# Full-array products for the sample tokens, and the sample states' updates from operands split into rounded halves

## The reference

```python
num   = einsum('btsh,bshv->bthv', qk, vc) + w_inter * einsum('bthk,bhkv->bthv', qc, C)   # within 8 tokens, plus the old state
C_new = sc_prev * C + einsum('bsh,bshk,bshv->bhkv', sc, kc, vc)                          # 128 x 256, one for each b and h
h     = rmsnorm(num / den) ; y = (h * gate) @ w_out
```

## Time and profile before

| | us |
|---|---|
| median of three runs | 2357.36 |
| the profiled execution, its own time | 2356.68 |
| its span, first to last instruction | 2354.9 |
| PE busy in it | 2318.1 (98%) |
| DVE busy | 1079.0 (46%) |
| ACT busy | 670.7 (28%) |
| POOL busy | 29.7 (1%) |

### The profile page before, as it was taken

The page is one execution under the profiler, slowest core; times in us unless marked ns, Lnnn a source line. Parts: engine busy times, 40 slices in busy tenths (PEclk is TensorE's granted clock), DMA queues, the critical chain, the costliest instruction groups (busy, mean ns, idle before and its releaser), DMA issues.

```text
span 2354.9 us, 39247 instructions
## 1 busy us (share of the span) xinstructions
PE 2318.1 (98%) x17176; PEld 2277.5 (97%) x17176; DVE 1079.0 (46%) x1395; ACT 670.7 (28%) x814; POOL 29.7 (1%) x20
## 2 busy tenths in 40 slices
PE   7999999999999999999999999999999999999997
PEld 7999999998989999999999999999988899999997
DVE  5333334684545433333543333354665454334245
ACT  4212222453423222212422222233322432222122
POOL 0000000000000000000000000000000100000000
PEclk9999999999999999999999999999999999999999
DMA  4222222233322222221222222222122222222221
GB/s 174 89 89 72 89 72 72 90 98 107 112 94 75 89 90 72 89 89 63 88 82 90 72 89 89 67 78 90 53 90 76 94 75 92 84 89 72 90 68 62
DMA packets 72551, 201.28 MB, mean 85 GB/s; under 512 B 7268, under 2 KB 26980, under 8 KB 72448
## 3 DMA queue, kind: packets, MB, share of 16 engines
q1 hardware_dynamic: 72448, 199.80, 26.4%
HBM read 187.82 MB, written 11.95 MB: 85 GB/s over the span
## 4 chain that ended last, share of the span: by engine, by line
PE 91%; DVE 4%; issue 3%; ACT 1%; POOL 0%; DMA 0%; DVEq 0%; SPq 0%; POOLq 0%; ACTq 0%
PE ps L443 82%; PE ps L668 3%; PE ps L523 1%; PE ps L710 1%; DVE w_lo L1508 1%; PE ps L688 1%; DVE og L1675 0%; PE ps L699 0%; PE ps L546 0%; PE ps L533 0%; PE ps L717 0%; PE ps L702 0%; DVE x L2159 0%; PE ps L494 0%; POOL scratch L1488 0%
## 5 line engine op out<-in xcount | busy, mean ns | idle before, releaser
L443 PE MATMUL ps<-xn_hi,w_hi 128*128 128x288 f32 x3328 | 718.9, 298 | 12.7 <-DVE w_lo L1508 11.5
L443 PE MATMUL ps<-xn_hi,w_lo 128*128 128x288 f32 x3328 | 713.0, 296 | 0.0
L443 PE MATMUL ps<-xn_lo,w_hi 128*128 128x288 f32 x3328 | 712.8, 296 | 0.0
L443 PEld LDWEIGHTS ps<-xn_hi,w_hi 128*128 128x128 f32 x3328 | 536.6, 189 | 21.9 <-DVE w_lo L1508 11.5
L443 PEld LDWEIGHTS ps<-xn_lo,w_hi 128*128 128x128 f32 x3328 | 536.6, 189 | 0.0
L443 PEld LDWEIGHTS ps<-xn_hi,w_lo 128*128 128x128 f32 x3328 | 536.6, 189 | 0.0
L1096 ACT ACTIVATE w_hi<-raw 128x1024 fp32r<-128x1024 f32 x332 | 331.4, 1046 | 361.1 <-PE ps L443 327.3
L1508 DVE TENSOR_TENSOR w_lo<-raw,w_hi 128x1024 fp32r<-128x1024 f32 x332 | 393.4, 1226 | 39.7 <-ACT w_hi L1096 37.6
L443 PE MATMUL ps<-h_lo,w_hi 128*128 128x288 f32 x1616 | 351.4, 297 | 2.6 <-DVE h_hi L1821 2.6
L443 PE MATMUL ps<-h_hi,w_hi 128*128 128x288 f32 x1616 | 351.8, 297 | 1.4 <-DVE w_lo L1508 1.4
L1553 DVE TENSOR_TENSOR scratch<-ps,rstd 128x576 f32<-128x576 f32 x88 | 66.6, 757 | 537.2 <-PE ps L443 534.2
(11 more groups left out here) (235 smaller groups left out, 1544.4 us busy)
## 6 DMA issues: line engine op xcount, KB each, us to landing
raw<-in_w_gate SPq DMA_DIRECT2D x88, 512.0 KB, 3.7
raw<-in_w_up SPq DMA_DIRECT2D x88, 512.0 KB, 4.5
raw<-in_w_down SPq DMA_DIRECT2D x64, 512.0 KB, 3.8
raw<-in_w_mix SPq DMA_DIRECT2D x64, 512.0 KB, 4.2
raw<-in_w_down SPq DMA_DIRECT2D x32, 384.0 KB, 3.6
state_s<-in_state_c SPq DMA_DIRECT2D x4, 1024.0 KB, 7.1
out_c_s<-state_s SPq DMA_DIRECT2D x4, 1024.0 KB, 4.5
state_s<-in_state_g SPq DMA_DIRECT2D x4, 1024.0 KB, 7.1
```

The source lines that it names most:

```text
L443: ins = nc.tensor.matmul(o, a, b[:, c] if c is not None else b, start=first and j == 0, stop=last and j == 2)
```

## The change

Three things are changed on PE, and the work that feeds them on ACT, POOL and DVE.

1. The 64 x 64 sample products become 128 x 128 or 128-row ones. The score block of `pairwise` is computed for 128 x 128 tokens, of which 64 x 64 are used. `sample_numerator` and `sample_den` contract over all 128 rows; the attention's rows 64 to 127 in those columns are zeros that POOL writes once for each mixer.
2. `sample_updates` takes float32r operands. ACT copies the 64 value rows, rounded, to both halves of a 128-row tile `vs_hi`; POOL writes the rest to the upper rows of `vs_lo`, whose lower rows are zero. POOL writes the keys rounded to rows 0 to 63 of `k_hl` and the rest to rows 64 to 127, and multiplies that by the mask over 128 rows. PE makes two matmuls for each sequence, by `vs_hi` and by `vs_lo`, instead of one float32 product.
3. `head_sums` makes two products of 288 columns instead of 512 and 64, and DVE reads both with one instruction instead of two.

```diff
-    batch = (s // DEC_SEQ == np.arange(DEC_BATCH)[None, :]).astype(np.float32)
+    batch = (s % SAMPLE // DEC_SEQ == np.arange(DEC_BATCH)[None, :]).astype(np.float32)
...
             def pairwise(bank, bank_s, left, right):
-                    ins = nc.tensor.matmul(ps[0:SAMPLE, bank_s, 0:SAMPLE], left[:, 0:SAMPLE],
-                                           right[:, 0:SAMPLE], start=True, stop=True)
+                    ins = nc.tensor.matmul(ps[:, bank_s, 0:P], left[:, 0:P], right[:, 0:P], start=True, stop=True)
...
             def sample_numerator(mixer, h, bank):
+                pe.wait_ge(att_zero, 3 * mixer + 2)
...
-                    nc.tensor.matmul(out, v_tok[0:SAMPLE, 0, vs], att(mixer, h)[0:SAMPLE, SEQ:TOK],
+                    nc.tensor.matmul(out, v_tok[:, 0, vs], att(mixer, h)[:, SEQ:TOK],
...
             def sample_updates(h, part, bank):
                 for b in range(4 * part, 4 * part + 4):
-                    ins = nc.tensor.matmul(ps[:, bank + (b % 4) // 2, (b % 2) * DV:(b % 2 + 1) * DV],
-                                           k_tok_b[:, b, :], v_tok[0:SAMPLE, 0, h * DV:(h + 1) * DV],
+                    out = ps[:, bank + (b % 4) // 2, (b % 2) * DV:(b % 2 + 1) * DV]
+                    nc.tensor.matmul(out, k_tok_b[:, b, :], vs_hi[:, :], start=True, stop=False)
+                    ins = nc.tensor.matmul(out, k_tok_b[:, b, :], vs_lo[:, :], start=False, stop=True)
...
             def head_sums(bank):
+                for c in range(2):
+                    ins = nc.tensor.matmul(ps[:, bank + c, 0:HALF_TOK], ones, cut2(T(5))[:, c, :],
...
-                    nc.tensor.matmul(den, ones[0:SAMPLE, :], att(0, h)[0:SAMPLE, SEQ:TOK], start=True, stop=False)
+                    nc.tensor.matmul(den, ones, att(0, h)[:, SEQ:TOK], start=True, stop=False)
...
+            def high_values(mixer, h):
+                u = N_HEADS * mixer + h
+                act.wait_ge(mx_free, MX_V[mixer][h])
+                if u:
+                    act.wait_ge(us_half, 2 * u)
+                    act.wait_ge(vs_lo_done, u)
+                for r in (0, SAMPLE):
+                    nc.scalar.activation(vs_hi[r:r + SAMPLE, :], v_tok[0:SAMPLE, 0, h * DV:(h + 1) * DV], ACT.Copy)\
+                        .then_inc(vs_hi_done, 1)
...
         def _(pool):
             for u in range(2 * N_HEADS):
+                pool.wait_ge(vs_hi_done, 2 * u + 2)
+                G.tensor_tensor(vs_lo[0:SAMPLE, :], v_tok[0:SAMPLE, 0, hs], vs_hi[0:SAMPLE, :].bitcast(f32), ALU.subtract)\
+                    .then_inc(vs_lo_done, 1)
                 pool.wait_ge(ktok_ready, u + 1)
+                G.tensor_copy(k_hl[0:SAMPLE, :], k_tok_s[:, :]).then_inc(pool_chain, 1)
+                pool.wait_ge(pool_chain, 2 * u + 1)
+                G.tensor_tensor(k_hl[SAMPLE:P, :], k_tok_s[:, :], k_hl[0:SAMPLE, :].bitcast(f32), ALU.subtract)\
+                    .then_inc(pool_chain, 1)
...
-                nc.gpsimd.tensor_tensor(k_tok_b[:, :, :], bcast_mid(k_tok_s[:, :], DEC_BATCH), bcast(batch, DK),
-                                        ALU.mult).then_inc(keys_b_done, 1)
+                G.tensor_tensor(k_tok_b[:, :, :], bcast_mid(k_hl[:, :].bitcast(f32), DEC_BATCH), bcast(batch2, DK),
+                                ALU.mult).then_inc(keys_b_done, 1)
...
-                    V.scalar_tensor_tensor(T(9)[:, 0:SAMPLE], ps[:, 7, 0:SAMPLE], 1.0 / DV, T(3)[:, 0:SAMPLE],
-                                           ALU.mult, ALU.add)
-                    V.scalar_tensor_tensor(T(9)[:, SAMPLE:TOK], ps[:, 6, :], 1.0 / DV, T(3)[:, SAMPLE:TOK],
+                    V.scalar_tensor_tensor(cut2(T(9)), ps[:, 6:8, 0:HALF_TOK], 1.0 / DV, cut2(T(3)),
```

More of the change, by code:

```diff
@@ L162, in program @@
         k_tok_s = sb("k_tok_s", [SAMPLE, DK])
-        k_tok_b = sb("k_tok_b", [SAMPLE, DEC_BATCH, DK])
+        k_hl = sb("k_hl", [P, DK], f32r)
+        k_tok_b = sb("k_tok_b", [P, DEC_BATCH, DK], f32r)
+        vs_hi, vs_lo = sb("vs_hi", [P, DV], f32r), sb("vs_lo", [P, DV], f32r)
         ps = ctx.enter_context(nc.psum_tensor("ps", [P, 8, 512], f32))
@@ L280, in program @@
         mx_done, mx_free, rt_done, rt_taken = (sem(n) for n in ("mx_done", "mx_free", "rt_done", "rt_taken"))
-        keys_b_done, hsq_sum = sem("keys_b_done"), sem("hsq_sum")
-        stage_done, stage_taken = sem("stage_done"), sem("stage_taken")
+        zero_done, keys_b_done, hsq_sum, vs_hi_done, vs_lo_done, pool_chain = (
+            sem(n) for n in ("zero_done", "keys_b_done", "hsq_sum", "vs_hi_done", "vs_lo_done", "pool_chain"))
+        att_zero, stage_done, stage_taken = sem("att_zero"), sem("stage_done"), sem("stage_taken")
         num_s_done, ht_s_ready, hsq_s_done, us_half, st_half = (sem(n) for n in (
@@ L709, in sample_updates @@
                 for b in range(4 * part, 4 * part + 4):
-                    ins = nc.tensor.matmul(ps[:, bank + (b % 4) // 2, (b % 2) * DV:(b % 2 + 1) * DV],
-                                           k_tok_b[:, b, :], v_tok[0:SAMPLE, 0, h * DV:(h + 1) * DV],
-                                           start=True, stop=True)
+                    out = ps[:, bank + (b % 4) // 2, (b % 2) * DV:(b % 2 + 1) * DV]
+                    nc.tensor.matmul(out, k_tok_b[:, b, :], vs_hi[:, :], start=True, stop=False)
+                    ins = nc.tensor.matmul(out, k_tok_b[:, b, :], vs_lo[:, :], start=False, stop=True)
                 ins.then_inc(us_half, 1)
             def head_sums(bank):
-                nc.tensor.matmul(ps[:, bank, :], ones, T(5)[:, SAMPLE:TOK], start=True, stop=True)
-                nc.tensor.matmul(ps[:, bank + 1, 0:SAMPLE], ones, T(5)[:, 0:SAMPLE], start=True, stop=True)\
-                    .then_inc(hsum_done, 1)
+                for c in range(2):
+                    ins = nc.tensor.matmul(ps[:, bank + c, 0:HALF_TOK], ones, cut2(T(5))[:, c, :],
+                                           start=True, stop=True)
+                ins.then_inc(hsum_done, 1)
             def mlstm_mix(ph):
@@ L1062, in last_down @@
                 sums(1)
+            pe.wait_ge(zero_done, 1)
             for ph in PHASES:
@@ L1378, in gla_mix @@
                 split_at(2)
+                high_values(1, 0)
                 for h in range(2):
@@ L1477, in _ @@
         def _(pool):
+            G = nc.gpsimd
+            G.memset(vs_lo[SAMPLE:P, :].bitcast(f32), 0.0).then_inc(zero_done, 1)
             for u in range(2 * N_HEADS):
-                pool.wait_ge(ktok_ready, u + 1)
+                if u % N_HEADS == 0:
+                    pool.wait_ge(rstd_ready, 2 if u == 0 else 5)
+                    for t in (1, 2) if u == 0 else (2, 3, 4):
+                        nc.gpsimd.memset(T(t)[SAMPLE:P, SEQ:TOK], 0.0).then_inc(att_zero, 1)
+                hs = slice(u % N_HEADS * DV, (u % N_HEADS + 1) * DV)
+                pool.wait_ge(vs_hi_done, 2 * u + 2)
+                G.tensor_tensor(vs_lo[0:SAMPLE, :], v_tok[0:SAMPLE, 0, hs], vs_hi[0:SAMPLE, :].bitcast(f32), ALU.subtract)\
+                    .then_inc(vs_lo_done, 1)
+                pool.wait_ge(ktok_ready, u + 1)
+                G.tensor_copy(k_hl[0:SAMPLE, :], k_tok_s[:, :]).then_inc(pool_chain, 1)
+                pool.wait_ge(pool_chain, 2 * u + 1)
+                G.tensor_tensor(k_hl[SAMPLE:P, :], k_tok_s[:, :], k_hl[0:SAMPLE, :].bitcast(f32), ALU.subtract)\
+                    .then_inc(pool_chain, 1)
+                pool.wait_ge(pool_chain, 2 * u + 2)
                 if u:
                     pool.wait_ge(us_half, 2 * u)
-                nc.gpsimd.tensor_tensor(k_tok_b[:, :, :], bcast_mid(k_tok_s[:, :], DEC_BATCH), bcast(batch, DK),
-                                        ALU.mult).then_inc(keys_b_done, 1)
+                    pool.wait_ge(keys_b_done, u)
+                G.tensor_tensor(k_tok_b[:, :, :], bcast_mid(k_hl[:, :].bitcast(f32), DEC_BATCH), bcast(batch2, DK),
+                                ALU.mult).then_inc(keys_b_done, 1)
                 pool.wait_ge(hsq_done, u + 1)
```

12 lines of the change are left out of this document (9 added, 3 removed).

## The result

| | before | changed |
|---|---|---|
| median, us | 2357.28 (4 runs) | 2327.62 (4 runs, 2324.51 to 2327.64) |
| the profiled execution, own time | 2356.68 | 2327.64 |
| its span | 2354.9 | 2325.9 |

The changed kernel is faster by 29.7 us: ratio 0.9866, 95% interval 0.9851 to 0.988. The prediction was 2329 in a range of 2322 to 2340.

What follows compares the result with a forecast made beforehand. PE was taken as the bound, busy 2318.1 of 2354.9 us. Savings of 15.8 + 4.7 + 5.5 + 0.5 + 1.5 = 28.0 us from 2356.68 gave 2328.7, with the median 0.7 higher: 2329, range 2322 to 2340.

Steps and rivals of the forecast that it cites:

- state updates: 16 parts on PE, each 1.21 us instead of 2.35; the last heads' save only through their first part: 15.8 us saved.
- score blocks: 20 sample score blocks on PE, each 1.28 us instead of 1.52: 4.7 us saved.
- numerators, denominators: Sample matmuls at 0.111 us each: 0.61 saved in 8 numerators, 0.16 in 4 denominators, together 5.5 us.
- head sums: Sums of 8 heads: 0.05 us saved in each, plus DVE's second instruction where a chain crosses it: 0.5 us.
- clock: PE's falls to 1.2 GHz in the mixers: 1.5 us saved, with ends at 4.5 saved and 3 lost.
- half of 0.111, as its columns would allow: Alternative price for the 48 64-column float32 matmuls in numerators and denominators: 2.7 us more saved; 0.111 was taken.
- What hides the added work: ACT's copies and POOL's steps before `sample_updates`: covered by 11.4 us in the tightest head, costing nothing on the path.
- The locks: DVE and POOL holding each other up through their shared port pair: booked at 0, 1.5 us either way.
- Not as said: Rival in the state updates: float32r matmuls run no faster than float32, updates give only the passage, 3 us: 2342; chance 0.04.
- Late operands: Rival: `sample_updates` waits for ACT's copies and four POOL steps in series, making the kernel slower: 2365; chance 0.03.

Runs made afterwards that it cites:

- the updates alone: Changed kernel with the padding of scores, numerators, denominators and the new head sums taken back, only state updates from split operands left: 2338.5 us, ratio 0.9922.
- the float32r one of 64 rows: Changed kernel with both matmuls of an update using only rows 0 to 63, the products of the keys' rest left out: 2331.60 us, one run.
- the changed kernel again: The changed kernel unaltered, measured once more beside two later versions: 2327.66 us, ratio 0.988.
- the padding alone: Kernel before with full-size score blocks, numerators and denominators, updates and head sums as they were: 2346.24 us, ratio 0.995.
- the float32 one of 128 rows: Changed kernel with state updates as plain float32 products zero-padded to 128 rows, without ACT's copies and POOL's splitting: 2334.83 us, one run.
- the last version: Changed kernel with DVE's last `low` earlier, the `k_tok_s` product padded, GLA head 3's level 0 inside a value tile: 2321.76 us, ratio 0.9849.

## Why the prediction was right

The sum was 28.0 us; the profiled executions differ by 29.0 and the medians by 29.7. Term by term:

| term | predicted | measured | from |
|---|---|---|---|
| state updates | 15.8 | 15.8 | start to start around each part in the updates alone; a part is 1.19 us where 1.21 was said |
| score blocks | 4.7 | 4.6 | 20 x 0.23 (1.48 to 1.25 in the GLA's) |
| numerators, denominators | 5.5 | 6.0 | 8 x 0.68, 4 x 0.15 |
| head sums | 0.5 | 0.8 | 8 x 0.10 |
| clock | 1.5 | 1.5 | 4 falls to 3 in the mixers, 1.5 each |
| sum | 28.0 | 28.7 | the two stretches gave 29.5 |

Of the 0.8 us between the last two, 0.6 is PE's wait for `kt`, 1.5 us before and 0.9 now, which the prediction didn't name. The runs tell with what it goes: it is 0.9 in the kernels that split the updates' operands on ACT and POOL (the updates alone, the float32r one of 64 rows, the changed kernel again) and 1.5 in those that don't (the padding alone, the float32 one of 128 rows). By what road isn't shown. PE's idle time in the mixers grew by 1.0 us for this reason, not by the 2 that were forecast: 1.6 more at the ends, 0.6 less here.

**The updates.** The new matmuls cost what those of the same shape and type cost in the value tiles, and the last head's parts paid only through the first: PE's wait grew from 1.3 to 2.1 us at each end, by 0.8 where 0.9 was said.

**The numerators** came out 0.5 us better in sum. A float32 matmul of 64 or 32 columns takes 1.26 / 12 = 0.105 us among full-size ones, a little under the 0.111 taken from those of 128 columns. The end of "half of 0.111, as its columns would allow" was never near: the block of 64 columns costs what that of 128 does.

**The head sums.** The scores behind the new sums take 1.23 us, behind the old ones 1.29 (the padding alone), as was said; the sums themselves got 0.05 shorter too, which was not in the sum.

**What hides the added work.** The term was nothing, and the trace has no wait of PE for it. But the cover in the tightest head, from the masking's end to its first use, fell from 9.5 to 3.7 us. The prediction's 11.4 runs from the masking's start: of these the series lost 1.9 by its later beginning (about 1 was said) and took 5.8 (5 to 7 was said).

**The locks.** They were booked at 0 with 1.5 us either way. One masking stood for 2.9 us (4.78 instead of 1.90), and three small POOL steps of one head took 1.2 to 1.3 us instead of 0.72, 0.28 and 0.45. Such meetings were not new: three of the eight maskings of the kernel before took 2.43, 2.94 and 3.13 us instead of 1.89. The subtraction that had taken 2.67 us on DVE takes 1.34 (at 1781.96), and none of the eight more than 1.38. No wait of PE grew with any of this.

**The clock.** The direction held, the account isn't borne out: the two falls that stood behind a numerator and denominator (636.17 and 683.96) went, as was said, but another came at 505.36, behind matmuls that the change doesn't touch, and one stayed at the mLSTM's end, where PE's wait had grown. The two are missing in the updates alone as well, where numerators and denominators are those of the kernel before, so that their shortening is not shown to be the reason. Four executions of the changed kernel in one set lie 4.6 us apart. A booking of one fall is within what the runs can't tell: that this term came out is luck.

**Two rivals were mispriced**, though neither decided anything. "Not as said" gave the passage 16 x 0.19 = 3 us. That sees one long interval too few at each end; it is 0.39 us a part, so that this case would have come out at 2339 and not at 2342. The kernel with float32 operands over 128 rows is that case: 2334.83 without a fall in the mixers, 2339.3 with the changed kernel's three. "Late operands" was to decide from 3.5 us of lateness in each of 8 heads and counted only the wait for the masked keys. With POOL's series 11 us longer, PE waited for the keys once, for 8.1 us, and the kernel was slower than before all the same: the squares' sum queued behind the masking and DVE's steps held up by it cost 18 us of waits, and the clock 9. The cover that counts on POOL is that of everything behind the masking in its list and of everything that runs on DVE meanwhile. The rival's size (2365) was met, its road was not.

## What to carry to other kernels

When a small product stands between full-size ones, read the interval before it and the two behind it as well as its own: the passage to a part of the array and back is paid by the neighbours, and padding to the full array with zeros removes it. In PE's time that costs nothing as long as the padded matmul has a price that doesn't grow with its columns, here up to 128 in float32. Where float32 products have 256 columns, sum them as float32r halves if another engine has cover to split the operands, and put both halves on the unused rows. Before work is added to an idle engine, count what stands behind it in its list and which two-input instructions of DVE run beside it, not only its consumer.

## What the runs showed of the hardware that was not expected

- A round trip from 128 rows of the array to 64 and back costs 0.39 us, the same for float32 and float32r. In float32r it is seen as four long intervals (0.21 and 0.23 in, 0.20 and 0.23 out, instead of 0.12).
- A float32 matmul of 256 columns takes 0.216 us from start to start, a float32r one 0.120, while float32 ones of 128, 64 and 32 columns all take 0.105 to 0.111. No run has a float32r matmul of 128 columns or fewer to set beside them.
- Three steps of POOL over 64 rows took 0.72, 0.28 and 0.45 us in one head and 1.23, 1.28 and 1.32 in another. The masking of 4.78 instead of 1.90 us at 1686.96 lay beside three two-input instructions of DVE, 0.74 and 2.35 us, together 3.1 against the 2.9 more: it seems that the two engines hold each other up in both directions. No run was made to separate the two.
- The clock doesn't always come back after 3.4 us, though PE is busy: from 503.2 in the updates alone, as in the padding alone and in the last version, it stayed at 1.2 GHz for 6.8 us with PE busy in all of them. The way to the first numerator was 2.8 us longer by it (90.2 against 87.4 us from the norm's sums, in the last version and the changed kernel again), where a fall of 3.4 us makes 1.5.
